# Six split slots and four raw ones in the expert stage, bias rows made in the route stage

## The chip, the cores and the metric

One Trainium2 chip, one core of it. The metric is the device time of one execution in microseconds (us). Engines are named as the profile names them: PE (matmuls), PEld (PE's weight loads), DVE (vector), ACT (scalar), POOL (GpSimd), SP (the queue that issues most DMAs); a q behind the name (SPq) is the engine's sequencer.

## The reference, cut to what matters

One layer of an encoder over 1,024 tokens (and 16 learned ones) of width 1,024, in float32. Two kinds of attention come first and fill `mixed`. What the change touches comes after it:

```python
h = h + mixed @ w_out                    # 1024 x 1024
v = rmsnorm(h) * g_ffn
top 4 of 32 experts of v @ w_router + b_router; gates = softmax over the four
a = v[tokens of e] @ w_mlp1[e] + b_mlp1[e]        # 1024 -> 2048, e of 32
y = swiglu_clamped(a) @ w_mlp2[e] + b_mlp2[e]     # 1024 -> 1024
h[token] += gate * y                     # the sum over a token's four experts
```

The second bias needs no expert to be run: for a token it is the row `gates (over 32 experts) @ b_mlp2`, a product of 32 terms.

## The kernel before, in words

Five stages follow each other: `project`, `attend_window`, `attend_diff`, `route`, `experts`. Between two of them all engines meet (the end of a Block). A float32 operand of a product is split in two float32r parts, high (ACT copies it) and low (DVE subtracts the high part from the original), and a product is three matmuls: high x high, low x high, high x low.

**`route`** (L1115 to L1497) goes over eight tiles of 128 tokens. In turn t PE turns tile t+1 of `mixed` (L1429), projects tile t in two halves of 24 matmuls each (L1441 to L1443), turns v of tile t-1 (L1453) and takes its logits (L1461), and counts ranks (L1467, L1468). DVE adds x (`residual`, L1321) into the two buffers `h2`, splits the turned `mixed` (L1307), normalises (L1327), picks the top four (`choose`, L1333 to L1342) and works out slots and gates (`place`, L1347 to L1359; its last result `dense_gates` holds a tile's gates over all 32 experts, three times side by side). SP stores `h2` to the output and v to `v_dram`. POOL scatters each (token, gate) to its slot in `slot_dram` by four indirect DMAs a tile (L1223), and waits for all of them at the end. After the last tile DVE and PE make the table of jobs (L1387 to L1497).

**`experts`** (L1501 to the end) runs one job after the other; a job is one expert with up to 256 of its tokens. All engines loop over `n` jobs with the same counters. A job is of kind "one" (up to 128 tokens), "few" (up to 192) or "two" (up to 256); the kind sets how many matmuls a weight piece gets: 12, 20 or 24. A job's weights are 12 pieces of 1 MB, [128, 2048] float32: eight of w_mlp1 (k = 0 to 7), four of w_mlp2 (8 to 11). A piece goes through two rings:

- SP loads it into one of RAW = 6 raw slots (four of them, `raw_first`, are loaded in `route` already), as soon as the piece six before it has been split (L1631 and L1632 wait on `hi_done` and `lo_done`);
- ACT and then DVE split it (L1732, L1845) into one of SPL = 4 slots of `whi` and `wlo`, once PE has used up the piece four before it (`w_used`). In step k of a job they split piece k + AHEAD, AHEAD = 3.

The order of work on ACT and on DVE is written out by hand in `body`. Between the splits of steps 0 to 11 DVE has: bias on the gate half (L1867, steps 2 and 6), the linear half with its clamp and product (L1872, L1857 and L1852, which makes `hh`; steps 3 and 7 in kind "one"), the low part of the turned `hh` (L1899, steps 6 and 8) and of the next job's turned tokens (L1904, step 10). PE turns `hh` (L2016) after pieces 5 and 8 and the next job's tokens (L1996) after piece 9. ACT has the gelu (L1738), the high parts (L1753, L1757) and, after the last piece, the gated output `ys` (L1776), and only then the next job's step 0. POOL gathers the next tokens (L1652), spreads the bias b1 (L1701) and adds `ys` to the output by indirect DMAs with an add (L1705).

**Ahead of the loop** `experts` does the second bias: PE turns the eight tiles of gates (L2111), ACT and DVE split them (L1819, L1973), ACT and DVE split three weight pieces (AHEAD), PE makes eight bias tiles of [128, 1024] (L2119), ACT and DVE copy them to eight buffers (L1824, L1979), POOL adds them to the output by eight DMAs with an add (L1670). SP loads the first job's slots (`idn`, L1621), POOL clears `xg` (L1661) and gathers its tokens (L1652), PE turns them (L1996), ACT and DVE split them (L1757, L1904), and the loop begins.

## Time and profile before

| | us |
|---|---|
| runs: median of 3 (lowest, highest) | 2428.54 (2428.15, 2431.27) |
| the profiled execution, its own time | 2426.24 |
| its span, first to last instruction | 2424.6 |
| PE busy | 2281.5 (94%) |
| DVE busy | 1874.5 (77%) |
| ACT busy | 1399.9 (58%) |
| POOL busy | 593.9 (24%) |
| DMA queue q1 (weights, inputs), share of 16 engines | 58.8% |

A share of the span is an average over stages with different limits, and matmuls are pipelined, so a busy PE is not PE at its peak. Route's steady turns lie from about 740 to 858 us, its end and the preparation of the experts from 858 to 917, the jobs from 917 to 2406.

### The profile page before, as it was taken

To read this page: it belongs to the slowest core of one execution; us is meant where nothing else is said; L and a number is where in the kernel's file an instruction comes from. 1 tells how busy PE (TensorE), PEld (TensorE's weight loads), DVE (VectorE), ACT (ScalarE), POOL (GpSimd) and SP (SyncE) were. 2 spreads that over 40 slices of the span, in tenths; PEclk is the share of its full clock that TensorE was granted. 3 is DMA by queue.
4 is the path that set the end of the run, shared out by engine and by line. 5 is a ranking of instruction groups with operands and counts; after the bars stand their busy time and mean duration, and the time that the engine had idled before them with its cause. 6 is when DMAs were issued, how large, how long until landed. Compare 5 with 4: busy or idle time off the path is not lost. (4 is left out here: it accounts for less than half of the span.)

```text
span 2424.6 us, 34957 instructions
## 1 busy us (share of the span) xinstructions
PE 2281.5 (94%) x10657; PEld 1715.7 (71%) x10658; DVE 1874.5 (77%) x2403; ACT 1399.9 (58%) x1672; POOL 593.9 (24%) x555
## 2 busy tenths in 40 slices
PE   6999699999998948999999999999999999999996
PEld 5778565555546836777777877777777777777875
DVE  4476455999966757889897589788888878989986
ACT  4322354888864436666675457565656555757755
POOL 0133000111110233324142113231133221423523
PEclk9999799899998958999999999999999999999999
DMA  5243730333105639889797669796889777979986
GB/s 161 64 122 97 154 65 22 99 71 70 36 1 158 106 123 317 319 285 341 268 371 243 200 234 362 275 319 224 268 288 313 241 236 245 370 245 364 376 293 225
DMA packets 251919, 519.68 MB, mean 214 GB/s; under 512 B 28657, under 2 KB 60657, under 8 KB 251809
## 3 DMA queue, kind: packets, MB, share of 16 engines
q1 hardware_dynamic: 229666, 480.01, 58.8%
q0 software_dynamic: 22176, 38.70, 7.0%
q8 instruction: 42, 0.69, 0.1%
q14 instruction: 35, 0.29, 0.0%
HBM read 493.06 MB, written 60.15 MB: 228 GB/s over the span
## 5 line engine op out<-in xcount | busy, mean ns | idle before, releaser
L1845 DVE TENSOR_TENSOR wlo<-raw_first,whi 128x2048 fp32r<-128x2048 f32 x259 | 618.6, 2406 | 115.4 <-ACT whi L1732 103.2
L1732 ACT CAST whi<-raw_first 128x2048 fp32r<-128x2048 f32 x259 | 489.3, 1907 | 144.4 <-PE gl_ps L2024 95.0
L2026 PE MATMUL gl_ps<-whi,xt_hi 128*128 128x512 f32 x1056 | 418.6, 396 | 16.2 <-DVE wlo L1845 7.8
L2028 PE MATMUL gl_ps<-whi,xt_lo 128*128 128x512 f32 x1056 | 412.4, 391 | 0.0
L2027 PE MATMUL gl_ps<-wlo,xt_hi 128*128 128x512 f32 x1056 | 412.2, 390 | 0.0
L1845 DVE TENSOR_TENSOR wlo<-raw_later,whi 128x2048 fp32r<-128x2048 f32 x128 | 292.1, 2282 | 57.2 <-ACT whi L1732 57.2
L1732 ACT CAST whi<-raw_later 128x2048 fp32r<-128x2048 f32 x128 | 240.9, 1908 | 65.7 <-PE gl_ps L2024 48.0
L2026 PEld LDWEIGHTS gl_ps<-whi,xt_hi 128*128 128x128 f32 x1056 | 198.7, 188 | 69.3 <-issue 11.9
L2028 PEld LDWEIGHTS gl_ps<-whi,xt_lo 128*128 128x128 f32 x1056 | 198.8, 188 | 42.9
L2027 PEld LDWEIGHTS gl_ps<-wlo,xt_hi 128*128 128x128 f32 x1056 | 199.0, 188 | 40.0
L1652 POOL DMA_INDIRECT xg<-v_dram,idn x67 | 123.4, 1841 | 402.6 <-PE t_ps L1996 318.4
L2026 PE MATMUL y_ps<-whi,ht_hi 128*128 128x512 f32 x512 | 206.5, 403 | 0.0
L2028 PE MATMUL y_ps<-whi,ht_lo 128*128 128x512 f32 x512 | 200.0, 391 | 0.0
L2027 PE MATMUL y_ps<-wlo,ht_hi 128*128 128x512 f32 x512 | 199.5, 390 | 0.0
L757 DVE CUSTOM_DVE_ANT_0 e<-s_ps,zero,meta_nm 128x1024 f32<-128x1024 f32 x128 | 163.5, 1278 | 11.7 <-DVE dsb L772 9.6
L2024 PE MATMUL gl_ps<-wlo,xt_hi 128*64 128x512 f32 x416 | 164.7, 396 | 0.0
L2023 PE MATMUL gl_ps<-whi,xt_hi 128*128 128x512 f32 x416 | 162.3, 390 | 0.0
L1705 POOL DMA_INDIRECT out_h<-ys,idc x64 | 126.8, 1981 | 122.1 <-ACT ys L1776 76.7
L685 ACT ACTIVATE e<-e,nm 128x1040 f32<-128x1040 f32 x128 | 149.1, 1165 | 9.5 <-DVE nm L757 8.4
L870 PE MATMUL o_ps<-pt,v_all 128*64 128x512 f32 (+1 forms) x288 | 139.0, 605 | 0.0
L484 PE MATMUL pp<-w_in_hi,ut_hi 128*128 128x512 f32 (+3 forms) x344 | 132.0, 384 | 2.4 <-DVE ut_lo L345 2.4
L1701 POOL PARTITION_BROADCAST b<-b x32 | 91.9, 2873 | 166.7 <-DMA b<-in_b_mlp 163.6
(282 smaller groups left out, 4045.4 us busy)
## 6 DMA issues: line engine op xcount, KB each, us to landing
raw_first<-in_w_mlp SPq DMA_DIRECT2D x260, 1024.0 KB
raw_later<-in_w_mlp SPq DMA_DIRECT2D x130, 1024.0 KB
k_st<-qk_dram SPq DMA_DIRECT2D x32, 260.0 KB, 7.4
xs<-in_x SPq DMA_DIRECT2D x16, 512.0 KB, 3.9
w_in_raw<-in_w_in SPq DMA_DIRECT2D x32, 256.0 KB
q_st<-qk_dram SPq DMA_DIRECT2D x32, 256.0 KB, 6.6
qk_dram<-qk_hi SPq DMA_DIRECT2D x24, 256.0 KB, 2.4
qk_dram<-qk_lo SPq DMA_DIRECT2D x24, 256.0 KB, 2.8
```

The source lines that it names most:

```text
L484: pe.matmul(out, ut_hi[:, k, cols(i)], whi[:, s, 0:w], start=(k == 0), stop=False)
L685: act.activation(e[:, n % 2, i, :], e[:, n % 2, i, :], ACT.Exp, bias=nm[:, k:k + 1], scale=-1.0, accum_out=total[:, n % 16, i:i + 1]).then ...
L757: dve.tensor_tensor_reduce(e[:, n % 2, i, 0:SEQ], S(i), zero[:, :], -1.0, meta_nm[:, (n // NT) % 2, at:at + 1], ALU.add, ALU.min, nm[:, k: ...
L870: ins = pe.matmul(o_ps[DV:P, :], vt, pt[0:r, g % 2, c, :], start=(c == 0), stop=(c == 8), skip_group_check=True)
L1705: pool.indirect_dma_start(out=sums[:, :], out_offset=bass.IndirectOffsetOnAxis(ap=idc[:, half, 0:1], axis=0), in_=ys[:, half, :], in_offse ...
L1732: act.copy(whi[:, k % SPL, :], raw(k)).then_inc(hi_done, 1)
L1845: dve.tensor_tensor(wlo[:, k % SPL, :], raw(k), whi[:, k % SPL, :].bitcast(F32), ALU.subtract).then_inc(lo_done, 1)
L2023: ins = pe.matmul(bank, xh[:, 1, kc, :], hi, start=start, stop=stop, skip_group_check=True)
L2024: ins = pe.matmul(bank[0:FEW], xh[:, 1, kc, 0:FEW], lo, start=False, stop=stop, skip_group_check=True)
L2026: pe.matmul(bank, xh[:, half, kc, :], hi, start=start, stop=False, skip_group_check=True)
L2027: pe.matmul(bank, xh[:, half, kc, :], lo, start=False, stop=False, skip_group_check=True)
L2028: return pe.matmul(bank, xl[:, half, kc, :], hi, start=False, stop=stop, skip_group_check=True)
```

## The change

In `route`: each tile's bias row is made there (`turn_gates`, `high_gates`, `low_gates`, `bias_row`) and added to the sums (`add_row`) before they are stored; the sums of tiles 0 to 6 now stay in `mixed`, in place of the tile that was read, and the last one in a buffer of its own; they are stored four turns later. The last tile's v is turned into free banks, ahead of `ranks`. At its end SP loads the first job's slots and POOL gathers its tokens. In `experts`: all bias work is gone, RAW is 4 (`raw_later` is gone), SPL is 6 and AHEAD is 5.

```diff
 def route(...):
-        h2 = sb("h2", [P, 2, D])
+        def h2(t):
+            return mixed[:, t, :] if t < NT - 1 else rows1.last[:, :]
+        def row_bank(u):
+            return o_ps[:, 0:2, :] if u in (NT - 3, NT - 1) else tm_ps[:, :, :]
+        def tv_bank(t, b):
+            return o_ps[:, 2 + b, :] if t == NT - 1 else tv_ps[:, :]
...
 SP
             for t in range(NT):
-                sp.wait_ge(h2_done, 2 * (t + 1))
-                sp.dma_start(sums[t * P:(t + 1) * P, :], h2[:, t % 2, :]).then_inc(h2_sem[t % 2], 16)
...
                 sp.dma_start(v_dram[t * P:(t + 1) * P, :], vs[:, t % 2, :]).then_inc(v_sem[t % 2], 16)
+                if t >= 4:
+                    store_sum(t - 4)
+            for u in range(NT - 4, NT - 1):
+                store_sum(u)
+            sp.wait_ge(scattered, 16 * NT * TOP_K)
+            sp.dma_start(rows1.idn[:, :, :], slot_dram[0:JOB, :].rearrange("(h p) c -> p h c", p=P)).then_inc(idx_first, 16)
+            store_sum(NT - 1)
+            sp.wait_ge(sums_stored, 16 * (NT - 1))
 POOL
+            pool.memset(rows1.xg[:, :, :], 0.0).then_inc(rows_set, 1)
...
-            pool.wait_ge(scattered, 16 * NT * TOP_K)
+            for i in range(2):
+                pool.wait_ge(v_sem[i], 16 * (NT // 2))
+            pool.wait_ge(rows_set, 1)
+            pool.wait_ge(idx_first, 16)
+            for half in range(2):
+                pool.indirect_dma_start(out=rows1.xg[:, half, :], ...).then_inc(rows1.x_landed[half], 16)
 ACT, start of turn t
+                if 3 <= t:
+                    high_gates(t - 3)
 DVE
+            def low_gates(u):
+                dve.wait_ge(gt_high, u + 1)
+                dve.tensor_tensor(gates_p[HIGH, u % 2, :], gt_ps[HIGH, :], gates_p[HIGH, u % 2, :].bitcast(F32), ALU.subtract
+                                  ).then_inc(gt_low, 1)
+            def add_row(u):
+                dve.wait_ge(row_ready, u + 1)
+                dve.wait_ge(v_done, u + 1)
+                dve.tensor_tensor(h2(u)..., row_bank(u), h2(u)..., ALU.add).then_inc(row_added, 1)
...
             for t in range(NT + 2):
+                if 3 <= t <= NT:
+                    low_gates(t - 3)
+                if 4 <= t <= NT - 1:
+                    add_row(t - 4)
                 if t < NT:
                     residual(t, 0)
...
+                if t == NT + 1:
+                    low_gates(NT - 2)
                 if t >= 2:
                     place(t - 2)
...
+                if t == NT:
+                    add_row(NT - 4)
+                    add_row(NT - 3)
                 if 1 <= t <= NT:
                     choose(t - 1)
...
             (the table of jobs)
+            add_row(NT - 2)
+            add_row(NT - 1)
 PE
             def transpose_mixed(t):
...
+                if t >= 5:
+                    pe.wait_ge(row_added, t - 4)
...
+            def turn_gates(u):          # one transpose, [128, 96]
+            def bias_row(u):            # two matmuls, 96 x 128 by 512 columns
...
                 project_out(t, 1, KC // 2, KC)
+                if t >= 3:
+                    bias_row(t - 3)
                 if t >= 1:
                     logits(t - 1)
+                if t >= 2:
+                    turn_gates(t - 2)
+            transpose_v(NT - 1, 0)
+            transpose_v(NT - 1, 1)
+            ranks(NT - 2)
+            bias_row(NT - 3)
+            logits(NT - 1)
+            turn_gates(NT - 2)
+            ranks(NT - 1)
+            bias_row(NT - 2)
...
 def experts(...):
-        RAW, SPL, AHEAD, OWN = 6, 4, 3, 3
+        RAW, SPL, AHEAD = first.SLOTS, 6, 5
-        later = sb("raw_later", [P, RAW - first.SLOTS, PK * 512])
...
 SP
-            for k in range(first.SLOTS, RAW):
+            load_bias(e0)
+            for k in range(RAW, AHEAD):
+                sp.wait_ge(hi_done, k - RAW + 1)
+                sp.wait_ge(lo_done, k - RAW + 1)
                 load(k, e0)
-            load_bias(e0)
             with sp.Fori(0, n) as j:
...
-                for k in range(RAW, NP + RAW):
+                for k in range(AHEAD, NP + AHEAD):
                     sp.wait_ge(hi_done, j * NP + (k - RAW + 1))
                     sp.wait_ge(lo_done, j * NP + (k - RAW + 1))
                     load(k, e if k < NP else nxt)
 POOL
-            pool.memset(xg[:, :, :], 0.0).then_inc(setup, 1)
-            pool.wait_ge(idx_first, 16)
-            for half in range(2):
-                gather(half)
...
-            for t in range(NT):
-                pool.wait_ge(b_copied[t % 2], t // 2 + 1)
-                pool.dma_start(sums[...], stage[t], accum_op=ALU.add).then_inc(b_stored[0 if t < 3 else 1], 16)
 ACT
-            act.wait_ge(gt_ready, 1)
-            act.copy(gates_p, t_ps[...]).then_inc(gt_copied, 1)
             for k in range(AHEAD):
                 split(0, k)
-            for t in range(0, NT, 2):
-                act.wait_ge(b_ready, t + 1)
-                act.copy(stage[t], bias_banks(t)).then_inc(b_copied[0], 1)
             keep_x0(0)
 DVE
-            dve.wait_ge(gt_copied, 1)
-            dve.tensor_tensor(gates_p[bias.HIGH], ...).then_inc(gt_low, 1)
             for k in range(AHEAD):
                 split(0, k)
-            for t in range(1, NT, 2):
-                dve.tensor_copy(stage[t], bias_banks(t)).then_inc(b_copied[1], 1)
             keep_x0(0)
-            dve.wait_ge(b_stored[0], 16 * 3)
 PE
-            (eight transposes of the gates, sixteen matmuls of the bias rows)
             transpose_x0(0)
-            for half in range(2):
-                pe.wait_ge(b_copied[half], NT // 2)
```

## Rows read from the trace of the kernel before

**Rows 1.** Busy time by stretch: us, then each engine, PEclk, DMA share, GB/s
```profile
740.00:858.00 118.00, 116.68 (x622) 98.68 (x622) 82.98 (x239) 44.98 (x75) 23.64 (x24) 0.98 0.56 126
...
858.00:917.00 59.00, 22.96 (x90) 16.70 (x90) 29.78 (x89) 18.65 (x22) 21.73 (x21) 0.52 0.48 144
...
921.40:2406.50 1485.10, 1461.09 (x6722) 1155.73 (x6721) 1258.11 (x980) 929.71 (x755) 441.55 (x319) 1.00 0.85 292
```

**Rows 2.** The same for single jobs: one "few", then two of kind "one"
```profile
1123.40:1182.20 58.80, 58.80 (x274) 45.30 (x273) 47.97 (x40) 32.70 (x30) 15.94 (x12) 1.00 0.76 266
2168.70:2205.50 36.80, 35.34 (x161) 28.34 (x160) 32.45 (x25) 26.41 (x19) 11.08 (x9) 1.00 0.94 319
2241.00:2276.50 35.50, 34.73 (x161) 28.56 (x160) 34.31 (x24) 26.52 (x19) 17.35 (x10) 1.00 1.03 373
```

**Rows 3.** Waits of PE, PEld and ACT in the loop: us in total, times, longest
```profile
PE t_ps L2016 <- DVE hh L1852: 13.0, 16, 0.9
PE gl_ps L2026 <- DVE wlo L1845: 7.8, 9, 3.6
...
PEld t_ps L2016 <- DVE hh L1852: 19.9, 17, 1.4
PEld gl_ps L2026 <- ACT whi L1732: 9.8, 16, 1.0
...
ACT whi L1732 <- DMA raw_first<-in_w_mlp: 1.4, 2, 1.2
```

**Rows 4.** Timeline of the job from 2205.5: DVE, then PE: start, us
```profile
2209.65 3.15 DVE L1845 TENSOR_TENSOR wlo<-raw_first,whi 128x2048 fp32r<-128x2048 f32 x1 [1.02 <-ACT whi L1732]
...
2219.51 6.69 DVE L1845 TENSOR_TENSOR wlo<-raw_first,whi 128x2048 fp32r<-128x2048 f32 x3
...
2230.69 0.69 DVE L1852 SCALAR_TENSOR_TENSOR hh<-sg,lin 128x512 f32<-128x512 f32 x1
...
2231.44 0.66 PE L2016 MATMUL t_ps<-ident,hh 128*128 128x128 f32 x4 [0.78 <-DVE hh L1852]
```

**Rows 5.** Timeline of SP in the same job: loads of weight pieces
```profile
2215.22 3.17 SPq L1616 DMA_DIRECT2D raw_later<-in_w_mlp  x2
```

**Rows 6.** Busy time of a slice of this job, columns as in rows 1
```profile
2205.50:2213.00 7.50, 7.50 (x34) 6.20 (x33) 6.48 (x4) 6.56 (x5) 6.22 (x2) 1.00 1.04 389
```

**Rows 7.** Timeline of the job from 1479.3: a load on SP, its split on ACT
```profile
1484.59 2.57 SPq L1616 DMA_DIRECT2D raw_first<-in_w_mlp  x2
...
1494.87 1.91 ACT L1732 CAST whi<-raw_first 128x2048 fp32r<-128x2048 f32 x1 [1.23 <-DMA raw_first<-in_w_mlp]
```

**Rows 8.** Route's end: L1115 on POOL's sequencer, the first slots' landing, gathers
```profile
L1115 POOLq DRAIN  x1: 2758/2758/2758, 886.9 to 886.9; - x1
...
DMA to landing us min/median/max: 1.9/1.9/1.9
...
894.18 1.01 POOL L1652 DMA_INDIRECT xg<-v_dram,idn  x1 [0.30 <-issue]
```

**Rows 9.** Route's last tile on DVE and PE: v, `place` of the tile before, logits, pick
```profile
861.53 1.28 DVE L1327 SCALAR_TENSOR_TENSOR vs<-h,rs,g_ffn_sb 128x1024 f32<-128x1024 f32 x1
...
867.84 0.82 DVE L1359 TENSOR_REDUCE dense_gates<-share 128x96 f32<-128x384 f32 x1
...
869.38 3.62 PE L1461 MATMUL r_ps<-w_router_sb,vt 128*128 128x32 f32 x16 [0.68 <-ACT vt L1263]
...
873.12 0.19 DVE L1333 TENSOR_TENSOR lg<-r_ps,b_router_sb 128x32 f32<-128x32 f32 x1 [4.45 <-issue]
```

**Rows 10.** Groups of DVE by line in route, 740 to 858
```profile
L1307 DVE TENSOR_TENSOR mt_lo<-tm_ps,mt_hi 128x1024 fp32r<-128x1024 f32 x7 | 8.6, 1222 | 6.7 <-ACT mt_hi L1240 6.7
```

**Rows 11.** Timeline of the experts' start: ACT, DVE and PE
```profile
893.62 5.50 ACT L1732 CAST whi<-raw_first 128x2048 fp32r<-128x2048 f32 x3
...
912.64 1.23 DVE L1904 TENSOR_TENSOR xt_lo<-t_ps,xt_hi 128x1024 fp32r<-128x1024 f32 x1 [1.53 <-ACT xt_hi L1757]
...
916.81 0.79 PE L2026 MATMUL gl_ps<-whi,xt_hi 128*128 128x512 f32 x1 [5.26 <-PEq L2070]
```

More of the change, by code:

```diff
@@ L1108, in _, with route @@
                     act.copy(ot[:, u % 2, :], o_ps[0:DV, :]).then_inc(ot_done, 1)
-def route(nc, a, mixed, gates, picks, jobs, bias, sums, v_dram, slot_dram, weights):
+def route(nc, a, mixed, gates, picks, jobs, rows1, sums, v_dram, slot_dram, weights):
     with ExitStack() as ctx:
@@ L1151, in route @@
         b2 = sb("b2", [3 * N_EXP, D])
+        b2_p = sb("b2_parts", [3 * N_EXP, D], F32R)
+        dense = sb("dense_gates", [P, 2, 3, N_EXP])
+        gates_p = sb("gates_parts", [3 * N_EXP, 2, P], F32R)
+        HIGH, LOW = slice(N_EXP, 2 * N_EXP), slice(2 * N_EXP, 3 * N_EXP)
         share = sb("share", [P, TOP_K, N_EXP])
@@ L1156, in route @@
         x_sem = [sem(f"x4_landed{i}") for i in range(2)]
-        h2_sem = [sem(f"h2_stored{i}") for i in range(2)]
         v_sem = [sem(f"v_stored{i}") for i in range(2)]
@@ L1253, in _ @@
             head_std(1)
-            for t in range(NT + 1):
+            for t in range(NT + 3):
+                if 3 <= t:
+                    high_gates(t - 3)
                 if t + 1 < NT:
                     copy_mt(t + 1)
-                if t >= 1:
+                if 1 <= t <= NT:
                     u = t - 1
@@ L1468, in ranks @@
                 pe.matmul(r_ps[:, 32:64], cst[:, C_TRI:C_TRI + P], sel[:, :], start=False, stop=True).then_inc(rank_ready, 1)
+            def turn_gates(u):
+                pe.wait_ge(dense_done, u + 1)
+                pe.wait_ge(vt_done, 2 * min(u + 2, NT - 1))
+                if u >= 1:
+                    pe.wait_ge(gt_low, u)
+                pe.transpose(gt_ps, dense[:, u % 2, :, :].rearrange("p i e -> p (i e)"), ident).then_inc(gt_ready, 1)
+            def bias_row(u):
+                pe.wait_ge(gt_low, u + 1)
+                if u == 0:
+                    pe.wait_ge(b2_low, 1)
+                if u < NT - 4:
+                    pe.wait_ge(mt_low, u + 5)
+                elif u == NT - 3:
+                    pe.wait_ge(h2_done, 2 * (NT - 1))
+                else:
+                    pe.wait_ge(row_added, NT - 2 if u == NT - 1 else NT - 3 if u == NT - 2 else u)
+                for c in range(2):
+                    ins = pe.matmul(row_bank(u)[:, c, :], gates_p[:, u % 2, :], b2_p[:, 512 * c:512 * c + 512], start=True, stop=True)
+                ins.then_inc(row_ready, 1)
             transpose_mixed(0)
-            for t in range(NT + 2):
-                if t < NT:
-                    project_out(t, 0, 0, KC)
+            for t in range(NT):
+                project_out(t, 0, 0, KC)
                 if t + 1 < NT:
@@ L1497, in _, with experts @@
             pe.matmul(r_ps[0:1, 128 + 2 * NJ:128 + 3 * NJ], ec[:, 2:3], ej[:, 2, :], start=True, stop=True).then_inc(cnt_ready, 1)
-def experts(nc, a, first, bias, jobs, v_dram, slot_dram, sums):
+            bias_row(NT - 1)
+def experts(nc, a, first, rows1, jobs, v_dram, slot_dram, sums):
     with ExitStack() as ctx:
@@ L1527, in experts @@
         b1 = sb("b1", [P, 2 * D])
-        idn = sb("idn", [P, 2, 2], U32)
+        idn = rows1.idn
         idm = sb("idm", [P, 2, 2], U32)
         idc = sb("idc", [P, 2, 2], U32)
-        ident = bias.ident
-        rows = sb("bias_rows", [P, OWN, 2, 512])
-        ys_parts = lambda half: ys[:, half, :].rearrange("p (c n) -> p c n", n=512)
-        stage = [sg[:, :, :], lin[:, :, :], hh[:, :, :], ys_parts(0), ys_parts(1), *[rows[:, i, :, :] for i in range(OWN)]]
+        ident = rows1.ident
         gl_ps = ps("gl_ps", [P, 2, 2, 512])
@@ L1538, in experts @@
         G, LIN = 0, 1
-        w_landed = [*first.landed, *[sem(f"w_landed{i}") for i in range(first.SLOTS, RAW)]]
+        w_landed = first.landed
         def raw(k):
-            s = k % RAW
-            return first.raw[:, s, :] if s < first.SLOTS else later[:, s - first.SLOTS, :]
-        setup = sem("setup5")
+            return first.raw[:, k % RAW, :]
         hi_done, lo_done, w_used = sem("hi_split"), sem("lo_split"), sem("w_used")
@@ L1636, in _ @@
                 load_bias(nxt)
-            for i in range(RAW):
-                sp.wait_ge(w_landed[i], n * 32 + 16)
+            for i in range(AHEAD - RAW):
+                sp.wait_ge(w_landed[i], n * (16 * NP // RAW) + 32)
+                sp.sem_inc(passed, 1)
+            for i in range(AHEAD - RAW, RAW):
+                sp.wait_ge(w_landed[i], n * (16 * NP // RAW) + 16)
+                sp.sem_inc(passed, 1)
             sp.wait_ge(b1_landed, n * 16 + 16)
@@ L2148, in build @@
                 attend_diff(nc, a, v_all, mixed, qk_dram, stacks, weights)
-            bias = BiasRows(nc, whole)
-            route(nc, a, mixed, gates, picks, jobs, bias, sums, v_dram, slot_dram, weights)
-        experts(nc, a, first, bias, jobs, v_dram, slot_dram, sums)
+            rows1 = FirstRows(nc, whole)
+            route(nc, a, mixed, gates, picks, jobs, rows1, sums, v_dram, slot_dram, weights)
+        experts(nc, a, first, rows1, jobs, v_dram, slot_dram, sums)
 def rope_table():
```

125 lines of the change are left out of this document (59 added, 66 removed).

## The prediction

> **What bounds the kernel now.** I read the page first, then the busy time by stretch, the same for single jobs, the waits of PE, and timelines where these pointed. The loop over the jobs is 1485 of 2425 us, with PE busy for 1461 of it and the DMA share at 0.85; the stretch from the end of route's turns to the first job (858 to 917) has PE busy for 23 of 59 us, at half clock [rows 1]. A "few" job is all PE: 58.80 of 58.80 us. A job of kind "one" is not. It takes 35.5 us, and in it PE is busy for 34.7, DVE for 34.3 and the DMA engines for all of it (share 1.03) [rows 2]. There are 13 "few" jobs, 18 "one" and one "two". Eight of the "one" jobs follow another "one" and have windows like the last of [rows 2]; nine follow a larger job, like the second, with share 0.94; the very first job is the other.
>
> PE's waits in the loop say which of the three ends last: 32.9 us on PE and its loads (partly the same time) for `hh` of DVE, 17.6 us for split weight pieces [rows 3]. The timeline of a "one" shows the circle: `hh` ends at 2231.4, PE turns it at once, does the last pieces, ACT can then store `ys` and start step 0's split, and DVE gets its only wait of the job there, 1.02 us at 2209.65; from there it works without a gap to the next `hh` [rows 4]. So in these jobs what DVE waits for between steps 0 and 7 moves the end of the job one for one.
>
> **Part 1, the two rings.** In step k ACT and DVE split piece k+5 instead of k+3, into six slots instead of four. The split waits until PE has used piece k-1, as before (k+3-4 and k+5-6 are the same). The load of piece p is issued when piece p-4 has been split, which now happens in step p-9, where p-6 was split before: issue stays where it was. Only the date changes by which the load must have landed: step p-5, not p-3. Four steps of time instead of six; the two steps lie behind the split now, where they help against a late split but not against a late load. ACT works in order, so a split that waits for its load holds gelu and `hh`'s high part behind it, and DVE behind that.
>
> How long may a load take? The load of piece 10 goes out at 2215.22, step 1 [rows 5]. Step 5, which must split it after the change, starts on DVE at 2219.51 + 2 x 2.2 = 2223.9 [rows 4], and ACT's 1.9 us come first. Left: 2223.9 - 1.9 - 2215.2 = 6.8 us. Before, it had six steps, some 13 us.
>
> How long does it take? No row gives a landing directly unless somebody waits. The lower bound: 1.05 MB at the 389 GB/s of a slice with full DMA engines is 2.7 us [rows 6], and a tiny load needs 1.9 us [rows 8], together 4.6 us (an estimate). The upper bound is a row where ACT did wait for a load: issued at 1484.59, split at 1494.87, 10.3 us [rows 7]. So a load is between 2.2 us early and 3.5 us late. In these jobs the engines are full [rows 2, 6], with three to four loads and POOL's output adds in the queues together, so the loaded end is the nearer one; with two loads ahead of it, 3 x 2.7 and part of the 1.9 make 8.8 us, 2.0 late. I take 2.0 us for each of the eight jobs: **+16 us**, ends 0 and 28. In a "few" job a step is 4.9 us and the DMA share 0.76, so four steps are 20 us and nothing is late. The nine that follow larger jobs start with full rings; 0, with an end at +1 each.
>
> The Trainium skill has a rule that speaks for the shorter window being harmless: by "DMA: Bandwidth & Descriptors", section "Anatomy of one DMA", a DMA takes about 2.0 us plus its bytes over 436 GB/s, an estimate of 4.4 us for a piece. By that rule the 6.8 us would do and the loop would lose nothing (the first rival's time). The 10.3 us of [rows 7] speak against using it where the queues are full.
>
> PE's 17.6 us of waits for pieces [rows 3] I count as no gain: one of 3.6 us is the loop's first return, and the rest falls in "one" jobs, where an earlier PE then waits for the same `hh`.
>
> **Part 2, route's turns.** PE gets two matmuls of 512 columns (0.23 us apart, as 144 of them and 16 transposes take 34.7 us in a job [rows 2]) in five turns and one transpose (0.15) in six: 5 x 0.46 + 6 x 0.15 = +3.2 us, since PE is busy for 116.7 of 118 us [rows 1]. DVE gets a subtraction on 32 partitions (0.3) and an add of [128, 1024] out of PSUM, like the 1.22 us of [rows 10], in four turns; it is busy for 83 of 118 us, so PE's slack covers it. If it were not covered, 5 x 1.5 = 7.5 us would stand in place of the 3.2. ACT's 0.3 a turn has cover (45 of 118 us). PE's new wait in `transpose_mixed` for `add_row`: 24 matmuls, 5.5 us, stand before it, against about 4 us for `choose`, the low part and the add. SP's new wait holds the next store and x load behind it, which are not due for a turn.
>
> **Part 3, route's end.** The last tile's v is turned before the ranks of the tile before and no longer waits for ACT between its halves. Logits ended with 869.38 + 3.62 = 873.0 [rows 9]. Now: v is ready at 862.8 as before, two times 1.1 us of transposes, ranks 0.9, bias row 1.2, logits 3.6: 870.7. DVE meanwhile has a low part and `place`, which ended at 868.7 before [rows 9], to 869.0, and two row adds to 871.4. The pick starts at 871.4, not 873.1: -1.7, and +0.3 for one more low part: -1.4. Two adds (2.4 us) behind the job table end with DVE at about 890, below POOL's path. That one decides: POOL passed its wait for the scatters at 886.9 and drained for 2.76 us before the engines met at 889.9 [rows 8]. Now SP's slot load (0.1 + 1.9) and POOL's two gathers (landing at 891.9, issued by 895.2: 3.3) come between: +5.3. Experts begin at 889.96 + 3.2 - 1.4 + 5.3 = 897.1.
>
> **Part 4, the experts' start.** Before: 889.96 to the first piece's matmul at 916.81 [rows 11], 26.85 us: turn the gates, split them, split three pieces, bias rows, turn and split the tokens, and 5.3 us of PE's sequencer. Now: table load 1.3, ACT's first high part 1.9 (5.50 for three with overlap), low part 2.3: 5.5; load 4 goes out at 5.7, lands by 4.6 more at 10.3; ACT 12.2, DVE 14.5, low part of the tokens 1.2 [rows 11]: 15.7, start at 15.9. DVE alone would have 3.2 + 5 x 2.2 + 1.2 = 15.4. PE's sequencer work lies beside it. -10.9 us; if load 4 takes 8.8, -6.7. The gathers of part 3 (landing within 7 us) are covered by the splits. The clock is at half level before and after. Parts 2 to 4: 3.2 - 1.4 + 5.3 - 10.9 = **-3.8 us**, ends -7 and +5.
>
> **The sum.** 2426.2 - 3.8 + 16 = 2438.4 us against the profiled execution. The median of the runs is 2.3 above that one, so the forecast for a median is 2441 us.
>
> **Rivals.** (a) Loads keep up in four steps (4.6 to 6.8 us, the rule's case), DVE stays the bound of "one": only parts 2 to 4 count, 2425 us. For it: ACT waited for loads for 1.4 us in the whole loop [rows 3]; against: it had six steps. (b) Faster: the two more split pieces do help. It happens where PE's 17.6 us for pieces [rows 3] are not followed by a wait for `hh`; the 3.6 of the first return stays, 14 us come back, and it decides if loads also keep up: 2411 us. Against: the 0.78 us wait of [rows 4] sits behind them. (c) The starvation feeds itself: every back-to-back "one" loses 3.5 and the nine others 1: 2428.5 - 3.8 + 28 + 9 = 2462 us. The ring of six may also simply not be deeper where it counts, as splitting is still released by PE's use of piece k-1; that is part of (a).
>
> **How the numbers follow.** Forecast 0.52, (a) 0.20, (b) 0.18, (c) 0.10. About 0.2% (4.9 us) is what a measurement here can tell from none. (a) lies at -0.16% and splits into 0.08 faster and 0.12 same; the forecast gives 0.05 to same. Faster 0.26, same 0.17, slower 0.57. The range 2412 to 2456 leaves out half of (b) and most of (c); the forecast's own is 2430 to 2456.
>
> **What would show it.** In the profile after: eight jobs of 37.5 us in place of 35.5, with ACT's `whi` waiting for "DMA raw_first" in some of them and PE's waits for `hh` up; PE's waits for pieces gone; route's turns 3 us longer; the engines meeting at 897; the first job at 913; "few" jobs at 58.8. Back-to-back jobs at 35.5 or less with no wait for a DMA would make it wrong.

## The result, and the profile after

| | before | after |
|---|---|---|
| median of the runs, us (lowest, highest) | 2428.57 (2428.15, 2431.27) | 2473.22 (2471.28, 2475.06) |
| profiled execution, its own time (span) | 2426.24 (2424.6) | 2472.12 (2470.5) |
| last add of x in route, us from the span's start | 857.8 | 873.0 |
| the engines meet, experts begin | 890.0 | 910.2 |
| first matmul of the first job | 916.8 | 927.8 |
| from there to the end of the span | 1507.8 | 1542.7 |

The ratio of the two is 1.0188, 95% interval [1.0176, 1.0200]: slower by 44.7 us, where 12 were forecast. The profiled executions differ by 45.9. By the marks in the table, +15.2 us come by the end of route's turns, +5.1 between them and the meeting, -9.2 in the experts' start, and +34.9 in the loop.

Busy time by stretch of the kernel after, columns as in [rows 1] (turns, experts' start, loop), then single jobs as in [rows 2]: a "few", a "one" after a larger job, and the three that follow it back to back:

```profile
738.80:873.00 134.20, 123.81 (x631) 104.47 (x632) 88.99 (x247) 45.62 (x80) 22.31 (x23) 0.93 0.38 95
...
910.20:927.80 17.60, 1.94 (x8) 1.57 (x8) 14.32 (x7) 13.29 (x8) 9.44 (x6) 0.50 0.61 195
927.80:2452.00 1524.20, 1475.76 (x6726) 1164.06 (x6727) 1268.57 (x979) 936.22 (x754) 443.19 (x316) 0.99 0.84 285
...
1144.60:1203.30 58.70, 58.70 (x273) 45.27 (x272) 48.08 (x40) 33.48 (x31) 15.45 (x11) 1.00 0.80 270
2203.10:2240.20 37.10, 35.29 (x162) 28.43 (x161) 32.51 (x25) 26.77 (x19) 12.74 (x10) 1.00 0.88 295
2240.20:2278.80 38.60, 35.06 (x161) 28.39 (x160) 35.83 (x24) 25.36 (x19) 13.55 (x11) 1.00 0.99 347
2278.80:2319.00 40.20, 36.48 (x161) 29.57 (x160) 36.22 (x24) 28.99 (x20) 15.36 (x11) 0.96 0.96 332
2319.00:2358.50 39.50, 35.50 (x161) 28.33 (x160) 35.22 (x24) 25.28 (x18) 15.12 (x11) 1.00 0.99 339
```

"Few" is where it was, and so, within 0.3 us, is the "one" after it. The back-to-back ones went from 35.5 us to 38.6, 40.2 and 39.5. Over the eight of them, from 37.2 to 40.6 us each, the loop lost 30.1 us, 3.8 a job. Of the other 4.8, jobs 2 and 3 (counted from 0: a "few" and the "one" behind it) have 4.0 together and three later ones about 1 each, and the first gained 1.5. The DMA share fell in the slow jobs, from 1.03 to between 0.96 and 0.99: the same weights now take a longer job.

The loop as a whole, first the kernel before, then after, with as many records of matmuls in both:

```profile
916.80:2424.60 1507.80, 1467.14 (x6736) 1160.24 (x6736) 1262.52 (x981) 933.54 (x758) 449.50 (x324) 0.99 0.84 289
...
927.80:2470.50 1542.70, 1478.32 (x6736) 1165.84 (x6736) 1275.98 (x981) 939.78 (x757) 450.55 (x321) 0.99 0.83 282
```

PE is busy for 11.2 us more with the same matmuls, so about a third of the 34.9 us is not waiting: PE works more slowly behind its pauses, as the windows below show. Summing the granted clock over PE's busy time gives an estimated 9.7 of the 11.2. The rest of the loss is idle time.

The waits in the loop, in total, times and longest, against [rows 3]:

```profile
DVE wlo L1922 <- ACT whi L1814: 192.4, 151, 5.2
...
ACT whi L1814 <- DMA raw_first<-in_w_mlp: 134.5, 127, 3.6
...
PE y_ps L2096 <- DVE ht_lo L1976: 20.9, 16, 3.6
...
PE t_ps L2086 <- DVE hh L1929: 12.1, 13, 1.0
```

ACT waited for a load twice before; now 127 times. PE's waits for low parts of pieces are gone from the head of the list. The longest in total is now one that the rows of before did not have: PE waits for `ht_lo`, 20.9 us. The timeline of one of these shows how it comes about, first ACT, then DVE, then PE:

```profile
2294.52 1.91 ACT L1814 CAST whi<-raw_first 128x2048 fp32r<-128x2048 f32 x1 [3.15 <-DMA raw_first<-in_w_mlp]
2297.12 1.91 ACT L1814 CAST whi<-raw_first 128x2048 fp32r<-128x2048 f32 x1 [0.69 <-DMA raw_first<-in_w_mlp]
2299.64 1.92 ACT L1814 CAST whi<-raw_first 128x2048 fp32r<-128x2048 f32 x1 [0.62 <-DMA raw_first<-in_w_mlp]
2301.46 0.58 ACT L1835 CAST ht_hi<-t_ps 128x512 fp32r<-128x512 f32 x1
...
2301.60 2.29 DVE L1922 TENSOR_TENSOR wlo<-raw_first,whi 128x2048 fp32r<-128x2048 f32 x1 [0.19 <-ACT whi L1814]
2303.81 0.68 DVE L1944 TENSOR_TENSOR sg<-gl_ps,b 128x512 f32<-128x512 f32 x1
2304.41 0.68 DVE L1976 TENSOR_TENSOR ht_lo<-t_ps,ht_hi 128x512 fp32r<-128x512 f32 x1
...
2305.23 0.77 PE L2096 MATMUL y_ps<-whi,ht_hi 128*128 128x512 f32 x1 [3.55 <-DVE ht_lo L1976]
```

Three splits in a row wait for their loads, 4.46 us in all. ACT works in its written order and copies `ht_hi` only behind them, DVE takes `ht_lo` only behind the third low part, and PE stands for 3.55 us. These pieces belong to a later part of the work; what PE lacked was one small copy behind them. Then a second price follows, in the same windows view:

```profile
2301.60:2305.20 3.60, 0.08 (x1) 0.00 (x0) 3.60 (x4) 3.02 (x4) 0.00 (x0) 0.94 1.06 392
2305.20:2307.00 1.80, 1.77 (x4) 1.50 (x5) 1.80 (x1) 1.75 (x1) 0.24 (x1) 0.50 1.05 387
2307.00:2310.00 3.00, 3.00 (x14) 2.44 (x13) 2.93 (x5) 1.91 (x1) 0.56 (x1) 0.80 1.00 329
```

After the pause PE ran at the lower of its two levels (1.2 instead of 2.4 GHz): 0.50 for 1.8 us and a mean of 0.80 over the next 3, an estimated 1.5 us more.

In route's turns the same pair, larger. PE's waits between 738 and 873, then the timeline where it stood, DVE ahead of PE, and the windows around it:

```profile
PE tm_ps L1557 <- issue: 7.0, 1, 7.0
PE o_ps L1506 <- DVE mt_lo L1348: 3.6, 1, 3.6
PE tm_ps L1494 <- DVE mixed L1410: 3.3, 2, 1.7
```

```profile
800.83 1.28 DVE L1365 SCALAR_TENSOR_TENSOR vs<-mixed,rs,g_ffn_sb 128x1024 f32<-128x1024 f32 x1
802.14 1.22 DVE L1440 TENSOR_TENSOR b_parts<-b,b_parts 32x1024 fp32r<-32x1024 f32 x1
...
803.46 1.19 PE L1557 MATMUL tm_ps<-b_parts,gates_parts 96*128 96x512 f32 x2 [7.05 <-issue]
```

```profile
795.00:803.00 8.00, 1.41 (x7) 0.81 (x5) 5.92 (x10) 3.59 (x6) 3.40 (x4) 0.78 0.23 34
803.00:812.00 9.00, 8.54 (x29) 7.51 (x30) 3.82 (x14) 0.45 (x3) 0.00 (x0) 0.50 0.45 88
```

The releaser is given as "issue", but the row of DVE that ends 0.10 us before PE starts names it: the low part of `b2_parts`, which DVE makes in turn 3 behind that turn's `normalise`, while PE wants it in the middle of the same turn for the first bias row. PE waits 7.05 us and then runs at half clock for the 9 us of the window, in which it does the work of 4.5.

At route's end and in the experts' start, POOL, SP, ACT and DVE:

```profile
895.75 0.95 POOL L1249 DMA_INDIRECT slot_dram<-code,dsti  x1 [0.30 <-issue]
904.17 1.05 POOL L1257 DMA_INDIRECT xg<-v_dram,idn  x1 [7.47 <-DMA idn<-slot_dram]
905.53 1.01 POOL L1257 DMA_INDIRECT xg<-v_dram,idn  x1 [0.30 <-issue]
...
900.74 0.43 SPq L1230 DMA_DIRECT2D idn<-slot_dram  x1
...
921.29 1.90 ACT L1814 CAST whi<-raw_first 128x2048 fp32r<-128x2048 f32 x1 [2.44 <-DMA raw_first<-in_w_mlp]
...
926.47 1.21 DVE L1981 TENSOR_TENSOR xt_lo<-t_ps,xt_hi 128x1024 fp32r<-128x1024 f32 x1
```

### The profile page after: what moved, and what is told of

It reads as the page before. It is cut to its first block and busy times, and to the rows that moved or that the text cites. A ratio compares the mean times of both kernels' runs of the same rounds, so it can differ in the third digit from the quotient of the medians.

```text
span 2470.5 us, 35018 instructions
## 1 busy us (share of the span) xinstructions
PE 2292.3 (93%) x10657; PEld 1721.7 (70%) x10658; DVE 1901.2 (77%) x2416; ACT 1408.1 (57%) x1677; POOL 595.2 (24%) x549
## 5 line engine op out<-in xcount | busy, mean ns | idle before, releaser
L1922 DVE TENSOR_TENSOR wlo<-raw_first,whi 128x2048 fp32r<-128x2048 f32 x389 | 927.3, 2400 | 213.8 <-ACT whi L1814 204.4
L1814 ACT CAST whi<-raw_first 128x2048 fp32r<-128x2048 f32 x389 | 739.4, 1907 | 350.7 <-PE gl_ps L2094 142.2
L1744 POOL DMA_INDIRECT xg<-v_dram,idn x65 | 125.0, 1923 | 440.0 <-PE t_ps L2066 397.6
L2096 PE MATMUL y_ps<-whi,ht_hi 128*128 128x512 f32 x512 | 209.4, 409 | 20.9 <-DVE ht_lo L1976 20.9
L1789 POOL DMA_INDIRECT out_h<-ys,idc x64 | 134.4, 2100 | 249.1 <-ACT ys L1858 196.2
L2096 PEld LDWEIGHTS y_ps<-whi,ht_hi 128*128 128x128 f32 x512 | 97.7, 191 | 47.2 <-issue 22.8
L485 PE MATMUL pp<-w_in_lo,ut_hi 128*128 128x512 f32 (+3 forms) x344 | 129.4, 376 | 0.0
L486 PE MATMUL pp<-w_in_hi,ut_lo 128*128 128x512 f32 (+3 forms) x344 | 128.3, 373 | 0.0
## 6 DMA issues: line engine op xcount, KB each, us to landing
raw_first<-in_w_out SPq DMA_DIRECT2D x2, 2048.0 KB, 12.1
```

Of the source, the lines that this page charges most:

```text
L1789: pool.indirect_dma_start(out=sums[:, :], out_offset=bass.IndirectOffsetOnAxis(ap=idc[:, half, 0:1], axis=0), in_=ys[:, half, :], in_offse ...
L1814: act.copy(whi[:, k % SPL, :], raw(k)).then_inc(hi_done, 1)
L1922: dve.tensor_tensor(wlo[:, k % SPL, :], raw(k), whi[:, k % SPL, :].bitcast(F32), ALU.subtract).then_inc(lo_done, 1)
L2096: pe.matmul(bank, xh[:, half, kc, :], hi, start=start, stop=False, skip_group_check=True)
```

## The experiments

**First: the forecast's steps apart.** The theory was now that the loop's loss is the raw window of four steps, and that route's is the one wait. The rivals: a longer look-ahead harms by itself; the bias rows' work is what route pays.

`b2_early`, the two parts of `b2_parts` one turn earlier:

```diff
-                if t == 2:
+                if t == 1:
                     act.wait_ge(b2_landed, 64)
...
-                if t == 3:
+                if t == 2:
                     dve.wait_ge(b2_high, 1)
```

> The changed kernel, with the two halves of the split of b_mlp2 made one turn earlier (ACT in turn 1, DVE in turn 2). Theory: in turn 3 PE's first bias row waited for the low part, which DVE made only behind normalise of the same turn; that stall (7.1 us) and the half clock behind it (some 4 us) are nearly all of the 15 us that route's turns got longer. Then this kernel ends 11 to 12 us earlier than the changed one: about 2461. Rival: the turns are longer because PE waits for add_row and has more matmuls in every turn, and the stall would only move to a later turn: 2469 or more.

2463.55 us, ratio to before 1.0143 [1.0124, 1.0161], 9.7 us less than after. The turns, from the first projection to the last add of x, took 125.0 us in place of 134.2 (before: 117.8). The wait is gone and little stepped into its place (the waits for DVE's adds rose from 3.3 us to 4.6). PE's waits in the turns are now:

```profile
PE tm_ps L1494 <- DVE mixed L1410: 4.6, 3, 1.7
PE o_ps L1506 <- DVE mt_lo L1348: 3.6, 1, 3.6
PE r_ps L1536 <- DVE sel L1380: 1.0, 1, 1.0
```

This run has the rings of after unchanged, and its loop took 1545.9 us in the profiled execution, against 1542.7. Loops with four raw slots thus differ by 3.2 us with the same rings, and a smaller difference between two single loops below says nothing. The six loops with six raw slots and a look-ahead of three, before's among them, lie between 1507.6 and 1509.4.

`rings_643`, the rings of before in the kernel after (the two added raw slots are a buffer `later`, as before):

```diff
-        RAW, SPL, AHEAD = first.SLOTS, 6, 5
+        RAW, SPL, AHEAD = 6, 4, 3
...
```

> The changed kernel with the rings of before (6 raw slots, 4 split slots, 3 pieces ahead); route is unchanged. Theory: the jobs lose time because a load has four steps to land where it had six. Then the loop, from the first matmul of job 0 to the end of the span, is back at 1507 to 1510 us (changed kernel 1542.7, before 1507.8), ACT waits for loads for under 5 us in place of 137, and the start of the jobs comes 2 to 5 us earlier with three splits in place of five: about 2435. Rival: the jobs lose through something else of the change (sums and first rows made elsewhere, the POOL queue's new order): the loop stays above 1530 and the time above 2458.

2432.71 us, ratio 1.0019 [1.0009, 1.0028]; the loop took 1508.6 us, before's 1507.8. Two back-to-back jobs, columns as in [rows 2]:

```profile
2210.00:2245.50 35.50, 34.70 (x162) 28.56 (x161) 34.29 (x24) 26.52 (x20) 17.20 (x10) 1.00 1.03 372
2245.50:2281.00 35.50, 34.70 (x162) 28.55 (x161) 34.27 (x24) 26.52 (x20) 17.08 (x11) 1.00 1.04 372
```

So all that the loop lost is in the rings: no other edit costs it anything that shows (0.8 us).

`rings_443`, the raw ring of four with the split ring and look-ahead of before:

```diff
-        RAW, SPL, AHEAD = first.SLOTS, 6, 5
+        RAW, SPL, AHEAD = 4, 4, 3
...
```

> The changed kernel with 4 raw slots, 4 split slots, 3 pieces ahead: two pieces less in all, but the same four steps from a load's issue to its date. Theory (the date of the load alone counts): the loop is as long as the changed kernel's, 1540 to 1546 us, although two split pieces fewer are held, and ACT waits for loads for 120 to 150 us. Rival (the number of pieces held in all counts): two fewer cost clearly more, over 1555. Second rival (the long look-ahead itself hurts, by putting waiting splits ahead of urgent work): shorter than 1535.

2457.74 us (one run), the loop 1532.6: a miss. Four raw slots cost 24 us and not all 34; ten belong to what is left, the six split slots or the look-ahead.

`half_loads`, where each load of the loop fetches half of its piece and the other half is old data:

```diff
-    sp.dma_start(raw(k).rearrange("p (k n) -> p k n", n=512), src)
+    sp.dma_start(raw(k).rearrange("p (k n) -> p k n", n=512)[:, 0:2, :], src[:, 0:2, :])
...
```

> The changed kernel with every weight load of the expert loop taking half of its piece (the other half of the slot keeps old data; the products are then of other numbers). Theory: all of the loop's loss is loads that land too late; at half the bytes a load takes 3 to 5 us, below the 6.8 us it may take, so ACT waits for loads for under 3 us and the loop is at or a little below before's 1507.8. Rival: order of work and split slots cost by themselves: the loop stays above 1520 with no wait for a load left.

2433.07 us (one run), the loop 1505.0. With quicker loads the rings of the change lose nothing, as expected. The expectation missed in one point: ACT's waits for loads stay at 25.9 us in 19, where under 3 were expected, and they cost nothing that shows. Only three of them are over 2 us, where after has 19 of its 129. My reading is that short waits are absorbed and long ones are not.

In this run 74 of the 96 splits of the back-to-back jobs did not wait for their load, and from a load's issue to its split it is 6.2 us in the median: that is the time that four raw slots leave a load.

**Second: the rest of route, and the ten microseconds.** `b2_643` is `b2_early` with `rings_643`.

> After, with b2_parts made a turn earlier and with the raw ring of six, split ring of four and look-ahead of three. If the two effects are independent: turns about 9 us shorter than in after, loop at 1507 to 1510 us, 2432.7 - 9.7 = about 2423 us, ratio to before 0.998. Rival (the gain of the earlier b2_parts came from something that the rings also take): above 2430 us.

2424.66 us, ratio 0.9982 [0.9972, 0.9991], where 2423 was expected: the two effects add up.

`rows_643` is `b2_643` with DVE's adds ahead of the pick and SP's slot load one store earlier:

```diff
-                if 4 <= t <= NT - 1:
-                    add_row(t - 4)
...
-                if t == NT:
-                    add_row(NT - 4)
-                    add_row(NT - 3)
+                if t >= 3 and t <= NT:
+                    add_row(t - 3)
                 if 1 <= t <= NT:
                     choose(t - 1)
...
-            for u in range(NT - 4, NT - 1):
+            for u in range(NT - 4, NT - 2):
                 store_sum(u)
...
+            store_sum(NT - 2)
             store_sum(NT - 1)
```

> As the run above, and in route DVE adds a bias row before it picks the top four of the same turn (so one turn earlier), and SP loads the first slots ahead of the store that waits for the last but one bias row. Theory: PE's waits for add_row ahead of its transposes (4.6 us in three) go, and SP's slot load, which went out at 900.7 in after, goes out some 5 us earlier, as soon as the last scatter has landed, and so does the meeting of the engines: together 7 to 9 us, about 2415 us. Rivals: the adds then hold up the pick and with it PE's ranks (turns no shorter); DVE's own end decides the meeting (no more than 2 us there).

2419.53 us, ratio 0.9965 [0.9953, 0.9978], 5.1 us less than `b2_643` where 7 to 9 were expected. The wait for the adds is out of PE's list, and the turns took 120.8 us in place of 124.6. The distance from the last add of x to the meeting hardly moved, 37.0 us against 37.3, but two effects cancel in it. The last scatter comes 23.9 us after the last add of x, where it came 22.8 after it: the adds now stand ahead of the pick, as the first rival had it (its turns did get shorter all the same). From that scatter to the meeting are 13.1 us in place of 14.5: the slot load goes out 4.1 us after the scatter was issued and no longer 5.0. SP's order thus brought some 1.4 us and not 5; the rest of the way the slot load waits for the scatter to land.

`gather_back` is `b2_643` with the first slots and tokens fetched in `experts`, as before:

```diff
 route
-            sp.dma_start(rows1.idn[:, :, :], slot_dram[0:JOB, :]...).then_inc(idx_first, 16)
...
 experts
+            sp.dma_start(idn[:, :, :], slot_dram[0:JOB, :]...).then_inc(idx_first, 16)
...
+            pool.wait_ge(idx_first, 16)
+            for half in range(2):
+                gather(half)
```

> As the first of these runs, but the first slots are loaded and the first tokens gathered in the experts stage, as before. Theory: route's end gets some 7 us shorter, the experts' start from their begin to the first matmul some 2 us longer (slots 2, gathers 5, transposes and splits of the tokens 4.5, beside three splits that took 11.2), so it is 4 to 6 us faster than the first of these. Rival: the gathers at route's end are worth what they were meant to be, and this is slower by 2 us or more.

2421.87 us, ratio 0.9978 [0.9969, 0.9988]. In the profiles route's end is 6.7 us shorter (30.6 against 37.3) and the experts' start 4.0 longer (15.2 against 11.2), where 2 were expected. With a look-ahead of three, fetching in `route` costs 2.7 us by these marks rather than bringing anything; the medians' difference of 2.8 agrees, but the intervals of the two ratios overlap, so the runs alone do not show it.

`rings_463` (`RAW, SPL, AHEAD = 4, 6, 3`):

> After with four raw slots and six split ones, but a look-ahead of three. A load has four steps of time here as in after and as with rings 4, 4, 3. If the ten microseconds between those two loops (1542.7 and 1532.6) come from the look-ahead of five, in that splits stand ahead of nearer work, the loop is at 1530 to 1534; if they come from the number of split slots (more pieces in flight), at 1541 to 1545.

2453.24 us (one run), the loop 1533.0, where `rings_443` had 1532.6. Two more split slots are worth nothing that shows, and the ten microseconds come with the look-ahead.

**Third: order on ACT, and the best version.** `rows_gather` has the four parts together (rings, `b2_parts`, adds, fetching back).

> Rings of six and four with a look-ahead of three, b2_parts a turn earlier, the bias row added before the pick, and the first slots and tokens fetched in the experts stage as before. From the two runs that had one of the last two each: route's turns as in rows_643 (4 us less than b2_643), route's end and the experts' start 2.6 us less than there: about 2418 us, ratio to before 0.996. Rival (both took the same time): 2420 us or more.

2420.22 us, ratio 0.9969 [0.9957, 0.9981]: faster than before, but not than `rows_643`. 2418 was expected, and 2420 or more was the rival by which both gains took the same time. The medians do not show a second gain. In the profiles route's end and the experts' start take 46.8 us together, where `rows_643` has 48.2: 1.4 us, half of what `gather_back` had brought.

`rows_gather_642` (look-ahead 2 there):

> The run above with a look-ahead of two. If every step of look-ahead stands in front of nearer work on ACT and DVE, and split pieces were never what PE waited for, the loop stays at 1507 us or gets shorter by up to 3 us, and the experts' start, bound by the tokens now, stays within 1 us. If two steps are too few for a split, PE waits for pieces in the jobs of kind one and the loop is 1515 us or more.

2507.44 us, ratio 1.0329 [1.0313, 1.0345], the loop 1597.8. My guess of a cost per step of look-ahead is wrong on this side. PE's waits turn to pieces:

```profile
PE gl_ps L2096 <- ACT whi L1814: 30.0, 12, 3.1
PE gl_ps L2096 <- DVE wlo L1922: 27.8, 18, 1.5
...
PE y_ps L2096 <- DVE wlo L1922: 19.9, 18, 1.1
```

`urgent_first`, after with ACT's gelu and both high parts of `hh` ahead of the split in jobs of kind "one":

```diff
+                    if kind == "one":
+                        if k in (2, 6):
+                            glu(j, k // 4, 0, kind)
+                        if k in (5, 8):
+                            keep_h(j, k // 8, 0, kind)
                     split(j, k + AHEAD)
+                    if kind == "one":
+                        continue
```

> After, with ACT's gelu and high part of the turned hh ahead of the split of the same step in jobs of kind one. If splits that wait for their loads do their harm by standing ahead of this work on ACT, PE's waits for ht_lo and for sg of DVE (20.9 and 7.8 us) fall by half or more and the loop is 8 us or more shorter than 1542.7. If the harm is that the pieces themselves come too late, the loop is within 3 us of it; if the split now waits too long for g_in and t_ready, it is longer.

2542.87 us (one run), the loop 1612.5, every "one" at 40 us or more. ACT's waits for loads fell to 26.8 us, and what took their place is worse: ACT waits for DVE's `sg`, and DVE for the split that ACT now holds behind it.

```profile
DVE wlo L1929 <- ACT whi L1814: 263.8, 187, 4.9
...
ACT sg L1820 <- DVE sg L1951: 128.0, 50, 4.1
```

This is the last branch of its expectation, and the run moved too much to tell between the first two.

**Fourth: what makes the loads late.** `rings_464` (`RAW, SPL, AHEAD = 4, 6, 4`):

> After with a look-ahead of four; four raw and six split slots stay. If each step of look-ahead beyond three costs by itself, the loop lies between the 1533.0 of a look-ahead of three and the 1542.7 of five: 1536 to 1540. If the cost comes from where step 5's split happens to stand (beside the high part of hh), it is 1533 or 1543, not between.

2476.99 us (one run), the loop 1546.8. That is not between 1533.0 and 1542.7, so a price for each step of look-ahead is out. Beside the 1545.9 of `b2_early` it cannot be told from a look-ahead of five: the other theory, by which the cost comes from where one split happens to stand, stays open.

`ht_first`, `urgent_first` with the one copy of step 8 alone:

```diff
+                    if k == 8 and kind == "one":
+                        keep_h(j, 1, 0, kind)
                     split(j, k + AHEAD)
...
```

> After, with only ACT's high part of the second half of hh (step 8 of a job of kind one) ahead of the split of that step, and nothing else moved. If the splits that wait for loads do the harm of the look-ahead by holding this copy, PE's wait for ht_lo (20.9 us) falls below 10 and the loop is 5 to 10 us shorter than 1542.7. If the wait only moves to the next piece or to hh, the loop stays within 2 us; if the split of step 8 now comes too late, it is longer.

2468.46 us (one run), the loop 1538.2, 4.5 us less than after and little more than the 3.2 by which two such loops differ. PE's wait for `ht_lo` only fell from 20.9 to 18.7 us, and that for `hh` rose from 12.1 to 15.2. The hold of that copy is how a late load reaches PE in some jobs; it is not what has to be taken away.

`few_adds`, after with the loop's output adds for one token only, so that the experts' sums are left out:

```diff
-                                            in_=ys[:, half, :], in_offset=None, bounds_check=SEQ - 1,
+                                            in_=ys[:, half, :], in_offset=None, bounds_check=0,
```

> After, with the loop's output adds done for the first token only, so that the sums of the experts are left out. It measures what the adds contribute to the late loads (the forecast put them into the loaded price of a load). If they are a main part, ACT's waits for loads fall from 137 us to under 60 and the loop is 15 us or more shorter; if the loads are late through their own number, the waits stay above 100 us and the loop is within 8 us of 1542.7.

2454.13 us (one run), the loop 1521.2. ACT's waits for loads in this run and PE's for `ht_lo`:

```profile
ACT whi L1814 <- DMA raw_first<-in_w_mlp: 122.3, 127, 2.4
...
PE y_ps L2096 <- DVE ht_lo L1976: 6.3, 14, 1.8
```

As many waits as in after, in total 15 us less (the same stretch of after, which begins with the experts' start here, has 137.3 us in 129), but none over 2.4 us instead of 3.6, and ten over 2 us instead of 19; the loop is 21.5 us shorter and PE's wait for `ht_lo` here fell by 14.6. The two conditions of the expectation did not hold together: the loop recovered as if the waits had gone, and nearly all of them stayed. What fits both is that the long waits count. `few_adds_463` and `few_adds_643` do the same edit in `rings_463` and `rings_643`:

> Rings of four raw and six split slots, look-ahead of three (loop 1533.0), with the output adds for the first token only (the sums of the experts are left out). If the look-ahead of five costs its ten microseconds by meeting the adds, this loop comes to that of few_adds, 1521.2, within 2 us. If the look-ahead costs apart from the adds, it keeps its distance: 1509 to 1514.

> The control: rings of six and four, look-ahead of three (loop 1508.6), with the output adds for the first token only. If the adds cost time only through late loads, the loop stays at 1506 to 1509. If leaving them out saves time by itself (POOL's ring of ys, the write of the sums at the end), it is 1500 or less, and 8 us or more of what few_adds saved is not the loads'.

The loops took 1519.7 and 1506.1 us, both as the first theory of their expectations has it. All six are single executions. The last column leaves out what comes behind PE's last matmul, where the last adds land:

| raw slots, look-ahead | loop, us | without the adds | the adds' part | of it, up to PE's last matmul |
|---|---|---|---|---|
| 6, 3 | 1508.6 | 1506.1 | 2.5 | 0.6 |
| 4, 3 | 1533.0 | 1519.7 | 13.3 | 11.5 |
| 4, 5 | 1542.7 | 1521.2 | 21.5 | 17.6 |

The adds cost the six raw slots next to nothing and the four a great deal. The other part of the loss is the four slots' own: without any adds they still cost 13.6 us (1519.7 against 1506.1). Without adds the look-ahead of five costs 1.5 us by the loops, 4.0 up to PE's last matmul, which is near the 3.2 of repetition; with them it is 9.7 and 10.1. So most of its ten microseconds, six to eight, come only together with the adds.

The landings agree. The issues' view of the jobs 27 to 29 gives the medians from issue to landing: first the kernel after, then `rings_463`, then `few_adds`:

```profile
raw_first<-in_w_mlp SPq DMA_DIRECT2D x36, 1024.0 KB, 7.6
out_h<-ys,idc POOLq DMA_INDIRECT x6, 10.0
```

```profile
raw_first<-in_w_mlp SPq DMA_DIRECT2D x36, 1024.0 KB, 7.0
out_h<-ys,idc POOLq DMA_INDIRECT x6, 9.2
```

```profile
raw_first<-in_w_mlp SPq DMA_DIRECT2D x36, 1024.0 KB, 6.9
out_h<-ys,idc POOLq DMA_INDIRECT x6, 7.3
```

Load by load (landing less issue, the 96 loads of the eight back-to-back jobs), with the time from issue to the split's start and the length of the loop:

| | landing median | slowest tenth above | issue to split, median | loop |
|---|---|---|---|---|
| before | 7.6 | 9.2 | 11.3 | 1507.8 |
| `half_loads` | 4.6 | 6.6 | 6.2 | 1505.0 |
| `few_adds` | 7.0 | 8.1 | 7.1 | 1521.2 |
| `rings_443` | 7.1 | 8.6 | 7.2 | 1532.6 |
| `few_adds_463` | 6.7 | 8.2 | 6.9 | 1519.7 |
| `rings_463` | 7.3 | 9.0 | 7.4 | 1533.0 |
| `ht_first` | 7.2 | 9.6 | 8.0 | 1538.2 |
| after | 7.4 | 9.7 | 7.5 | 1542.7 |
| `b2_early` | 7.6 | 10.2 | 7.7 | 1545.9 |
| `rings_464` | 7.5 | 10.7 | 7.6 | 1546.8 |

With six raw slots a load has 11.3 us and its landing time does not show. With four the split mostly starts as the load lands, and the eight rows with whole loads and four raw slots stand in the order of their slowest tenth and of their loop alike, but for one pair that is 1.5 us apart. That is an agreement between rows and no proof, and no even one: from 8.1 to 8.6 the loop grows by 11.4 us, from 8.6 to 9.0 by 0.4. In after the slow ones are pieces 8 to 10 (9.6, 9.8, 8.9 us in the mean), issued in steps 11, 0 and 1, when POOL adds the job before to the output; in `few_adds` the same three have 7.1, 7.1 and 6.6. Why the adds hit a look-ahead of five harder than three is not settled by these runs.

## Why the prediction was wrong in size

**What bounds the kernel**: right. "Few" stayed at 58.7 us, the back-to-back "one" jobs took the loss, and the nine after larger jobs lost little. `rings_643` gave the 35.5 back.

**Part 1, the rings**: the mechanism was right, the price was not. This is the step that failed: "I take 2.0 us for each of the eight jobs". It measured 3.8 us for each of the eight. The row of 10.3 us in [rows 7] and the landing time were well read: 8.8 us was taken, the measured loads have a median of 7.4 and a slowest tenth above 9.7. The window was read a little long: 6.8 us, where `half_loads` shows 6.2. What failed is the count. I priced one late load a job, but every load has the same four steps, and 85 of these 96 were split within 0.15 us of their landing, ACT waiting for them. That a job pays for the worst chain in it, as with the three held splits in the timeline above, is a reading of such timelines and not shown for every job. Two terms were at nothing without a reason. One is PE's lower clock behind its pauses: 11.2 of the loop's 34.9 us are busy time of the same matmuls. The other is the tail: landing times vary by several microseconds and the sum takes one value for them, into which it also counted the adds; the adds alone cost 21.5 us. That four raw slots and a look-ahead of five cost 15.1 us without any adds (1521.2 against 1506.1), near the forecast's 16, is chance and no support for it. Rival (c), with its 3.5 us a job, was the nearest; it had 0.10.

The Trainium skill's rule ("DMA: Bandwidth & Descriptors", section "Anatomy of one DMA") gives an estimated 4.4 us for a piece, by which the window would do. The page fits it to DMAs that GpSimd issues, and these loads go out on SP. The trace does not agree with it here: the shortest of the 96 loads took 5.0 us and the median 7.4. With half of the bytes the median was 4.6, and then the window did suffice.

That PE's waits for pieces bring no gain is borne out as far as a run shows it: in `half_loads`, where the longer look-ahead meets quick loads, the loop is 2.8 us shorter than before, and not the 14 of rival (b).

**Part 2, the turns**: +3.2 forecast, +16.4 from the first projection to the last add of x (134.2 against 117.8; the first projection itself came 1.2 earlier, which makes the +15.2 above). The work of PE was priced right: in `rows_643`, with both waits out, the turns took 120.8 us, +3.0. Two steps failed. The first: I did not look at who makes `b2_parts`. The change moves ACT's copy to turn 2 and DVE's low part to turn 3 (from 3 and 4), behind `normalise`, and in that same turn PE wants the row of tile 0; the new wait on `b2_low` is in the whole kernel's diff, and it stands in none of my sums. It cost 7.05 us and an estimated 4.5 of clock; taking it out brought 9.2 us in the turns and 9.7 by the median of `b2_early`. The second: "24 matmuls, 5.5 us, stand before it, against about 4 us for `choose`, the low part and the add". This cover was too thin, the wait came to 3.3 us in two turns, 4.6 in three once the larger wait was out, and taking it out brought 3.8. The upper end of 7.5 counted the work of DVE uncovered, not a wait.

**Part 3, route's end**: the pick's gain was right. The last scatter comes 22.7 us after the last add of x, where it came 24.3 after it: -1.5 against -1.4. The rest measured +6.6 against 5.3 (from the last scatter to the meeting 14.5 us, before 7.9): from SP's slot load to POOL's first gather are 3.4 us, where I had 2.0 for issue and landing; and POOL's drain behind the gathers is 3.7 us, where it was 3.1 behind the scatters. The gathers themselves were cheaper, 2.4 us and not 3.3. Together +5.1, not +3.9.

**Part 4, the experts' start**: -9.2 against -10.9. The fifth piece was split from 921.29, 11.1 us after the meeting, where I had 10.3 for its load. DVE ended the low part of the tokens at 927.7, 17.4 us after the meeting in place of 15.7, and the first matmul came with it.

The forecast's sum for parts 2 to 4 was -3.8 and came out at +11.1; part 1 gave +34.9 for 16. The time lies above the range's upper end of 2456, since the ends of part 1 (28 at the most) stopped below what it cost, and the ends of parts 2 to 4 (+5) had no place for a wait that was overlooked.

## What to carry to other kernels

How far ahead a load runs is set by the slots that it lands in: slots moved from raw to split data lengthen the look-ahead on paper and shorten the time a load has, here from 11.3 us to 6.2. Price that against the slow tenth of the landings under the real queues, not one landing, and over all loads in a row. And go through every new wait in a diff for its producer's place in its own engine's order: the one that was skipped here cost more than all the work that the change added to that stage.

## What the runs showed of the hardware

Two things I had not expected. A pause of 3.55 us of PE was followed by 1.8 us at the lower clock level and some more in the next 3 us, and one of 7.05 by 9 us, so the two waits cost an estimated 0.4 and 0.6 of their own length again. And a job's output adds of [128, 1024] took loads that were in the queues beside them from 7.1 to 9.8 us (piece 9, `few_adds` against after), with a ring that left no room for it; with six raw slots the same adds cost the whole loop 2.5 us (single executions).
